# The first eight up blocks of three MLPs written out ahead of their loop, in a kernel of two stacked blocks

## What is computed

```python
def sq_relu_mlp(h, w_up, w_down):
    return jnp.square(jax.nn.relu(h @ w_up)) @ w_down

# in each layer
h = h + mixer(rms_norm(h, g_mix[layer]))
h = h + sq_relu_mlp(rms_norm(h, g_mlp[layer]), w_mlp_up[layer], w_mlp_down[layer])
```

## Time and profile before

| | us |
|---|---|
| three runs | 1204.01, 1204.05, 1211.54 |
| median | 1204.05 |
| the profiled execution's own time | 1203.87 |
| its span, first to last instruction | 1202.1 |

### The profile page before, as it was taken

The page is one execution under the profiler, slowest core; times in us unless marked ns, Lnnn a source line. Parts: engine busy times, 40 slices in busy tenths (PEclk is TensorE's granted clock), DMA queues, the critical chain, the costliest instruction groups (busy, mean ns, idle before and its releaser), DMA issues.

```text
span 1202.1 us, 26288 instructions
## 1 busy us (share of the span) xinstructions
PE 1188.4 (99%) x9584; PEld 1152.8 (96%) x9584; DVE 829.9 (69%) x1422; ACT 710.9 (59%) x1309; POOL 197.3 (16%) x260
## 2 busy tenths in 40 slices
PE   9999999999999999999999999999999999999997
PEld 8898999999999999999999999999999999999886
DVE  5788886555557977565559968555557988666764
ACT  5657756564444556664447877665445697666343
POOL 4000014220000113220020003221102811232000
PEclk9999999999999999999999999999999999999999
DMA  9314336655557566656565426656555644765650
GB/s 295 99 39 136 104 95 199 198 175 185 191 184 228 177 197 188 196 189 206 183 207 184 161 76 212 200 186 208 176 176 178 208 141 144 225 197 188 201 184 36
DMA packets 194698, 208.87 MB, mean 174 GB/s; under 512 B 6103, under 2 KB 183352, under 8 KB 194488
## 3 DMA queue, kind: packets, MB, share of 16 engines
q1 hardware_dynamic: 192256, 202.78, 53.2%
q10 hardware_dynamic: 2360, 5.00, 1.3%
HBM read 206.69 MB, written 2.64 MB: 174 GB/s over the span
## 4 chain that ended last, share of the span: by engine, by line
PE 89%; DVE 5%; ACT 4%; issue 2%; DMA 0%; ACTq 0%; DVEq 0%
PE PS L1962 24%; PE PS L1964 23%; PE PS L1963 23%; PE PS L2557 2%; PE PS L2559 2%; PE PS L2558 2%; PE PS L1968 1%; PE PS L2190 1%; PE PS L2212 1%; DVE wlo L1122 1%; ACT whi L559 1%; PE PS L2146 1%; PE PS L2086 1%; PE PS L2320 1%; PE PS L2319 1%
## 5 line engine op out<-in xcount | busy, mean ns | idle before, releaser
L1122 DVE TENSOR_TENSOR wlo<-raw,whi 128x1024 fp32r<-128x1024 f32 x368 | 458.6, 1252 | 262.4 <-ACT whi L559 260.8
L559 ACT ACTIVATE whi<-raw 128x1024 fp32r<-128x1024 f32 x368 | 387.1, 1055 | 247.8 <-PE PS L1964 180.5
L1962 PE MATMUL PS<-x,whi 128*128 128x256 f32 (+2 forms) x1568 | 443.5, 283 | 0.1
L1963 PE MATMUL PS<-x,whi 128*128 128x256 f32 (+2 forms) x1568 | 438.7, 280 | 0.0
L1964 PE MATMUL PS<-x,wlo 128*128 128x256 f32 (+2 forms) x1568 | 438.1, 279 | 0.0
L1962 PEld LDWEIGHTS PS<-x,whi 128*128 128x128 f32 x1568 | 295.3, 188 | 2.1 <-issue 1.3
L1964 PEld LDWEIGHTS PS<-x,wlo 128*128 128x128 f32 x1568 | 295.8, 189 | 0.0
L1963 PEld LDWEIGHTS PS<-x,whi 128*128 128x128 f32 x1568 | 295.2, 188 | 0.5
L1963 PE MATMUL PS<-hid,whi 128*128 128x256 f32 (+1 forms) x768 | 214.0, 279 | 0.0
L1962 PE MATMUL PS<-hid,whi 128*128 128x256 f32 (+1 forms) x768 | 214.0, 279 | 0.0
L1964 PE MATMUL PS<-hid,wlo 128*128 128x256 f32 (+1 forms) x768 | 213.5, 278 | 0.0
(11 more groups left out here) (313 smaller groups left out, 1647.1 us busy)
## 6 DMA issues: line engine op xcount, KB each, us to landing
raw<-in_mlp_w SPq DMA_DIRECT2D x64, 1024.0 KB, 5.5
raw<-in_w_mlp_up SPq DMA_DIRECT2D x32, 1024.0 KB, 5.7
raw<-in_w_mlp_down SPq DMA_DIRECT2D x32, 1024.0 KB, 5.3
raw<-in_w_in_conv SPq DMA_DIRECT2D x12, 1024.0 KB, 5.1
raw<-in_attn_w_in SPq DMA_DIRECT2D x12, 1024.0 KB, 5.1
raw<-in_mlstm_w_in SPq DMA_DIRECT2D x12, 1024.0 KB, 5.3
raw<-in_w_in_attn SPq DMA_DIRECT2D x8, 1024.0 KB, 8.5
raw<-in_w_out_attn SPq DMA_DIRECT2D x4, 1024.0 KB, 4.9
```

Of the source, the lines that this page charges most:

```text
L559: A(part_view(whi, b), raw_view(b), ACT.Copy).then_inc(w_hi, 1)
L1122: V.tensor_tensor(part_view(wlo, b), raw_view(b), f32(part_view(whi, b)), ALU.subtract).then_inc(w_lo, 1)
L1962: mm(dst, whi_b, xs_hi, start=first, stop=False)
L1963: mm(dst, whi_b, xs_lo, start=False, stop=False)
```

## The change

In MLPs 1, 2 and 3 the first turn of PE's up loop is written out ahead of the loop. It begins with `linear_first` (new for MLPs 1 and 2). Behind it stands one wait, for `w_used` to count block 1 of the phase, that is for PE's own last product. Blocks 2 to 7 follow, then a loop over the other three turns, all with `linear` and without waits for x. In MLP 3 the turns 1 to 3 thus no longer start side by side. MLP 0 is written differently and does the same as before. The other engines' instructions are unchanged.

```diff
             def mlp(m, tok):
                 up, dn = f"up{m}", f"dn{m}"
-                with pe.Fori(0, FB // 8) as i:
-                    if m == 0:
-                        linear_first(up, xh, xl, tok, x_blocks(1), i * 8, 2)
-                    if m == 3:
-                        linear_first(up, *x_parts(7), tok, x_blocks(7), i * 8)
-                    for j in range(0 if 0 < m < 3 else 2, 8):
-                        linear(up, j, *x_parts(2 * m + 1), tok, x_blocks(2 * m + 1) if j == 0 else None, i * 8)
+                xs = x_parts(2 * m + 1)
+                if m == 0:
+                    with pe.Fori(0, FB // 8) as i:
+                        linear_first(up, *xs, tok, x_blocks(1), i * 8, 2)
+                        for j in range(2, 8):
+                            linear(up, j, *xs, tok, None, i * 8)
+                else:
+                    linear_first(up, *xs, tok, x_blocks(2 * m + 1))
+                    pe.wait_ge(w_used, B[up] + 2)
+                    for j in range(2, 8):
+                        linear(up, j, *xs, tok)
+                    with pe.Fori(1, FB // 8) as i:
+                        for j in range(8):
+                            linear(up, j, *xs, tok, None, i * 8)
                 if m == 0:
                     norm(1, tok[1])
                 else:
```

## The result

The changed kernel is slower: the ratio of its runs to those of the kernel before is 1.0065, with a 95% interval of 1.0043 to 1.0087. Its median is 1215.7 us (20 runs, 1207.4 to 1221.8), that of the kernel before 1211.6 (20 runs, 1203.9 to 1216.6). I had forecast 1205.1. That is within 1%, as forecast, but 8.5 us over my range. Both medians say little by themselves, because the runs of both kernels lie on levels. Before: 8 runs at 1203.9 to 1204.4, one at 1208.0, 8 at 1211.5 to 1212.9, 3 at 1215.7 to 1216.6. Three runs in all count as slow and are in no figure of this document: one of 4020 us (experiment 6), one of 3044 us (experiment 7) and one of 1223.2 us of the kernel before.

The account below looks back on a forecast made before the run. PE was taken as the bound, losing nothing in the changed phases. 1203.87 us (profiled execution) - 0 saved + 3 x 0.40 for pauses = 1205.1 us; range 1203.8 to 1207.2.

Parts of the forecast that it names:

- The side-by-side start: Start of MLPs 1 and 2: more slack for the last x piece, gain 0 in the profiled execution.
- the code and its fetch: Rival: fetching 576 more written-out products shows as 5 packets, 5.2 us, giving 1210.3 us; chance 0.04.
- the ring: Rival: weight ring slots come free late, block 4 waits 0.28 us in MLPs 1 and 2; 1205.6 to 1206.2, chance 0.03.
- the loop's entry: First PE step across the up loop's entry: 0.11 to 0.12 us expected; more would show code fetch.
- block 4's low part: Low weight part in MLPs 1 and 2, delayed by block 0's later end; expected in time, costed at 0.
- The pause: PE runs empty after product 48 in MLPs 1, 2 and 3: 0.40 us each, 1.2 us in all.
- Completion and release: At the new wait: 0.28 us until product 48 counts, 0.14 us until product 49 starts, 0.42 together.
- The refill: Behind the wait, the next product follows after 0.20 us instead of 0.11, 0.09 more.
- and then the beat of 0.1133 again: Behind the pause, PE returns to 0.1133 us a product to the phase's end; phase 87.4 us instead of 87.04.
- the pause's bounds: One pause costs at least 0.17 us and at most 0.93 us; over three, 0.5 to 2.8 us.
- the base: Profiled execution of the kernel before, 1203.87 us, with the median of its runs only 0.18 us above.
- What is not there cannot be saved: In the 3 x 768 up products of MLPs 1 to 3, PE loses nothing to waits or loop branches.

Follow-up runs that it names:

- experiment 6: Changed kernel without its wait, one 512-column product added ahead of block 2 in MLPs 1 to 3: 11 runs from 1204.7 to 1205.9 us, ratio 0.9969.
- experiment 7: Changed kernel with its wait naming block 0's count instead of block 1's: median 1208.5 us, ratio 0.9998 to the kernel before.
- experiment 1: Changed kernel without PE's wait for its own last product: 12 runs from 1203.8 to 1211.7 us, ratio 0.999 to the kernel before.
- 12: Changed kernel without its wait, 512-column products added in three mixers' last projections and ahead of block 2 of MLPs 1 to 3: median 1205.5 us, ratio 0.9964.
- 3: Changed kernel, wait kept, blocks 0 and 1 one after the other instead of side by side: median 1214.7 us, ratio 1.0058.
- experiment 2: Changed kernel with the wait in MLP 1 alone: median 1213.2 us, ratio 1.0040 to the kernel before.
- 8: Changed kernel without its wait, one 64-column product added ahead of block 3 in MLPs 1 to 3: median 1220.9 us, ratio 1.0086.
- 4: Changed kernel, waits kept, one 64-column product added ahead of block 3 in MLPs 1 to 3: 6 runs at 1222.4 to 1223.6 us, ratio 1.0125.
- 11: Changed kernel without its wait, three 512-column products added in the mixers' last projections: median 1205.0 us, one run at 1212.2, ratio 0.9976.
- 5: Changed kernel, waits kept, one 512-column product added ahead of block 3 in MLPs 1 to 3: median 1206.8 us, ratio 0.9983.
- 9: Kernel before, up loops unchanged, three 512-column products added in the mixers' last projections: median 1204.8 us, one run at 1212.2, ratio 0.9969.
- 10: Kernel before with 512-column products added in three mixers' last projections and each turn of MLP 0's up loop: median 1205.9 us, ratio 0.9987.

## Why the prediction was wrong

**Right.** Nothing was saved: without the wait the times are those of the kernel before (experiment 1). The side-by-side start, the code and its fetch (q8 54 packets against 50 in the earlier trace rows), the ring and the loop's entry cost nothing. ACT's first read in MLP 1 moved as forecast, to 5.38 us after the start, and block 4's low part was ready in time:

```profile
455.11 0.38 ACT L619 ACTIVATE act_r<-PS 128x256 f32<-128x256 f32 x1 [2.95 <-PE PS L1964]
...
456.76 1.22 DVE L1122 TENSOR_TENSOR wlo<-raw,whi 128x1024 fp32r<-128x1024 f32 x1 [0.23 <-ACT whi L559]
```

The pause was 0.33 us instead of 0.40, three times 1.0 instead of 1.2. Completion and release together took 0.33 us instead of 0.42; which of the two was shorter the rows don't show. The refill was 0.22 to the second product, against 0.20.

**Wrong, first and above all: "and then the beat of 0.1133 again".** This is the step that failed. I let PE return to its old step by itself behind the pause and priced the pause as a gap, with bounds from gaps. The step behind the pause is another quantity, and it is multiplied by all products up to the next break: 1,538 in MLP 1. 4.44 ns x 1538 = 6.8 us is 20 times the gap. Nothing in the sum could reach it, so the range, set by the pause's bounds, was too narrow by its kind. In the profile, MLP 1 has 3.5 + 3.6, MLP 2 0.6 and MLP 3 3.5 us of it, 11.2 of the 11.5; the second mixer's end is 0.7 longer too, but its stalls ahead of that were as much shorter (629.32 to 736.01 before, 636.64 to 743.38 after, 106.7 each).

**Wrong, second: the base.** I took the 0.18 us between the profiled run and the median of three as the spread of the runs. The third run, 1211.54, stood in the table, 7.5 us up. It was not noise but a level: 1,742 or 1,757 products at 4.44 ns more. Of 20 runs only 8 are at the level of my base.

**Wrong, third: "What is not there cannot be saved", read from phases without a gap.** True for the execution at hand, but MLP phases at 117.8 ns have no gap either, and with the wide products of experiments 6 and 12 the levels that they make are gone. A look at another stage of the profile before could have warned. In its score stage two blocks of the same shape stand within 5 us:

```profile
664.20 0.28 PE L1964 MATMUL PS<-x,wlo 128*128 128x256 f32 x1
...
666.24 0.28 PE L1964 MATMUL PS<-x,wlo 128*128 128x256 f32 x1
...
667.30 0.28 PE L1963 MATMUL PS<-x,whi 128*128 128x256 f32 x1
...
669.54 0.28 PE L1964 MATMUL PS<-x,wlo 128*128 128x256 f32 x1
```

From the first to the second are 18 steps in 2.04 us, 113.3 ns; from the third to the fourth 19 in 2.24 us, 117.9 ns.

What the text calls **shown**: that the wait, as a pause, is the cause (experiments 1, 3, 7); that the step is kept over the norm products and the loop branches (the down half); that the slow step needs no wait (2, 8); that PE went from 113.3 to 117.8 right at a narrow product (three times, 4 and 8) and from 117.8 to 113.3 right behind a wide one (three times, 11 and 12); and that with a wide product in each of MLPs 1 to 3 no run stood on a higher level (35 runs of 5, 6 and 12, all under 1208).

What is only **argued** is the mechanism under it, the lead of the weight load. In the trace each load starts with the product ahead of it at either step (2 to 5 ns behind its start), so it cannot show a lead. It does show two small differences: at the slow step a product is 281 ns long instead of 276 (its end is modelled), and one load in three takes 192 ns instead of 188. The Trainium skill (TensorE: Matmul & The Clock Gate, Back-to-back issue gap) says that in a stream of load and matmul pairs the spacing is set by both together, and gives N / 2.4 + 2.5 ns for a matmul alone, which is an estimate of 109.2 at 256 columns. The trace agrees that the pair is slower than that, 113.3 or 117.8.

**Open**: what decides the step behind a pause. It is not an even draw. Of the 13 pauses in the profiles of the changed kernel and of experiments 2 to 5, five were reached at 117.8, and all five led to 113.3; eight were reached at 113.3, and five of them led to 117.8, three to 113.3. In experiment 2, whose only pause is that of MLP 1, none of the 12 times is below 1210.8. Open is also why the step can change where nothing pauses. In the third mixer of every profile it does so where the products change their form, here in the kernel before:

```profile
929.62 0.28 PE L2457 MATMUL PS<-whi,x 128*128 128x256 f32 x1
...
930.64 0.28 PE L2457 MATMUL PS<-whi,x 128*128 128x256 f32 x1
930.76 0.28 PE L1962 MATMUL PS<-x,whi 128*128 128x256 f32 x1
...
932.88 0.28 PE L1962 MATMUL PS<-x,whi 128*128 128x256 f32 x1
```

That is 9 steps of 113.3 ns up to 930.64 and 18 of 117.8 from 930.76. Last, open is what set one run in twelve of 9 and of 11, and three of 10, up by 7.7 us or more: in these three the wide products stand in the mixers ahead of MLPs 1 to 3 (in 10 in MLP 0 as well) but not in these MLPs, and in 5, 6 and 12, which have one in each of these MLPs, no run did so.

## What to carry to other kernels

On an engine that is busy throughout, read the step between equal instructions, stage by stage, and compare stages of one shape: a share of 99% hides 4%. When an edit makes PE run empty, even for a third of a microsecond, the price may be not the gap but the step that follows, times the products up to the next break. And where runs of one kernel stand on levels, work out which stretch times which step makes the distance, before one profiled execution is taken as the base.

## What the hardware showed that I had not expected

- Products of 128 x 256 with a weight load each have two steady steps, 113.3 and 117.8 ns, both at a granted clock of 1.00. Each was kept for over 1,500 products, across loop branches and across the two norm products between up and down half. A pause reached at 117.8 led to 113.3 five times of five, one reached at 113.3 led to 117.8 five times of eight.
- One product of 512 columns was followed by 113.3 ns in all 21 places profiled among products of 256 columns (experiments 5, 6 and 9 to 12), three of which PE had reached at a steady 117.8, and with six of them 12 of 12 runs lay within 0.3 us. One product of 64 columns was followed by 117.8 in all six MLPs profiled in experiments 4 and 8, three of which PE had reached at 113.3.
- A wait for PE's own count cost 0.33 us, apart from the step behind it, where it named the last product, and nothing where it named one that started 0.34 us earlier.
- Products with 258 columns ran at 120 ns in every profile, with or without a wide product ahead.
